# Rounding weight chunks two slots at a time in a one-core float32 decoder block

## The reference

```
def conv_gated_mlp(h, w_up, conv_w, conv_b, w_down):
    up = h @ w_up
    up = causal_depthwise_conv(up, conv_w) + conv_b
    gate, val = jnp.split(up, 2, axis=-1)
    return (jax.nn.silu(gate) * val) @ w_down

def reference(x, mem, ...):
    x = first_block(x, mem, w_in, w_out, ...)   # rmsnorm, attentions, recurrence, feed-forward
    return second_block(x, ..., w_in_2, ..., w_up_2, ..., w_down_2)   # mixers, feed-forward
```

## Time and profile before

| what | value |
| --- | --- |
| median of 3 runs | 2844.6 us |
| profiled execution: span from its first to its last instruction | 2844.7 us |
| TensorE busy with matmuls | 2734.1 us, 96% |
| VectorE, ScalarE, GpSimd busy | 64%, 43%, 9% |
| mean granted TensorE clock | 0.986 of full speed |
| DMA | 171 GB/s mean, 51.4% of 16 engines in the weights' queue |

### The profile page before, as it was taken

The page is one execution under the profiler, slowest core; times in us unless marked ns, Lnnn a source line. Parts: engine busy times, 40 slices in busy tenths (PEclk is TensorE's granted clock), DMA queues, the critical chain, the costliest instruction groups (busy, mean ns, idle before and its releaser), DMA issues.

```text
span 2844.7 us, 54953 instructions
## 1 busy us (share of the span) xinstructions
PE 2734.1 (96%) x21630; PEld 2679.8 (94%) x21630; DVE 1818.3 (64%) x2392; ACT 1235.6 (43%) x1532; POOL 252.6 (9%) x181
## 2 busy tenths in 40 slices
PE   7999969999999999999999999899899999999997
PEld 7989969998999999999999999889899999999997
DVE  6555785654544676867674547997576767676444
ACT  4344554434433444444443434534444444444332
POOL 3000001230001100000000304510310000000010
PEclk9999989999999999999999999999999999999998
DMA  6555423556534555555555555445455555555553
GB/s 214 193 178 162 151 67 134 194 179 192 185 127 154 178 179 185 178 188 180 177 190 182 184 185 162 146 162 173 133 163 187 183 178 185 182 184 182 184 185 105
DMA packets 131704, 485.67 MB, mean 171 GB/s; under 512 B 14765, under 2 KB 14773, under 8 KB 131152
## 3 DMA queue, kind: packets, MB, share of 16 engines
q1 hardware_dynamic: 129744, 474.01, 51.4%
q0 software_dynamic: 1792, 9.18, 0.9%
HBM read 481.02 MB, written 2.11 MB: 170 GB/s over the span
## 4 chain that ended last, share of the span: by engine, by line
PE 88%; DVE 7%; ACT 2%; issue 1%; POOL 1%; DMA 0%; ACTq 0%; SPq 0%; DVEq 0%; POOLq 0%
PE ps L1535 88%; DVE w_lo L919 2%; DVE acc L1348 1%; ACT w_hi L560 1%; DVE op_lo L965 1%; DVE hbuf L1504 1%; DMA raw<-in_weights 0%; DVE x_res L1507 0%; POOL sqb L495 0%; POOL sumsq L484 0%; POOL sumsq_w L484 0%; DVE proj L937 0%; POOL sqb L482 0%; DVE r_c L1099 0%; ACT hbuf L892 0%
## 5 line engine op out<-in xcount | busy, mean ns | idle before, releaser
L919 DVE TENSOR_TENSOR w_lo<-raw,w_hi 128x1024 fp32r<-128x1024 f32 x900 | 1129.3, 1263 | 926.4 <-ACT w_hi L560 924.1
L560 ACT ACTIVATE w_hi<-raw 128x1024 fp32r<-128x1024 f32 x900 | 951.0, 1060 | 1315.8 <-PE ps L1535 1287.6
L1535 PE MATMUL ps<-op_hi,w_hi 128*128 128x256 f32 x5024 | 1436.9, 286 | 54.8 <-DVE op_lo L965 28.3
L1535 PE MATMUL ps<-op_lo,w_hi 128*128 128x256 f32 x5024 | 1428.2, 284 | 0.0
L1535 PE MATMUL ps<-op_hi,w_lo 128*128 128x256 f32 x5024 | 1428.1, 284 | 0.0
L1535 PEld LDWEIGHTS ps<-op_hi,w_hi 128*128 128x128 f32 x5024 | 971.6, 193 | 61.8 <-DVE w_lo L919 47.4
L1535 PEld LDWEIGHTS ps<-op_lo,w_hi 128*128 128x128 f32 x5024 | 971.4, 193 | 0.8 <-issue 0.2
L1535 PEld LDWEIGHTS ps<-op_hi,w_lo 128*128 128x128 f32 x5024 | 971.0, 193 | 0.0
L1535 PE MATMUL ps<-g_lo,w_hi 128*128 128x256 f32 x1408 | 398.5, 283 | 0.0
L1535 PE MATMUL ps<-g_hi,w_lo 128*128 128x256 f32 x1408 | 397.8, 283 | 0.0
L1535 PE MATMUL ps<-g_hi,w_hi 128*128 128x256 f32 x1408 | 394.7, 280 | 0.0
(11 more groups left out here) (252 smaller groups left out, 1801.6 us busy)
## 6 DMA issues: line engine op xcount, KB each, us to landing
raw<-in_weights SPq DMA_DIRECT2D x900, 512.0 KB, 3.8
x_res<-in_x SPq DMA_DIRECT2D x1, 2048.0 KB, 8.3
x_res<-in_x POOLq DMA_DIRECT2D x1, 2048.0 KB, 7.8
mem_x<-in_mem POOLq DMA_DIRECT2D x1, 2048.0 KB, 10.3
out_x<-x_res POOLq DMA_DIRECT2D x8, 256.0 KB, 2.3
rel_rev<-rel_dram POOLq DMA_DIRECT2D x1, 1024.0 KB, 7.4
hg_con<-in_hg_consts POOLq DMA_DIRECT2D x1, 576.0 KB, 4.0
par<-in_params POOLq DMA_DIRECT2D x1, 546.0 KB, 9.4
```

The costliest lines, as they stand in the source:

```text
L560: nc.scalar.activation(w_hi[:, s], raw[:, s], ACT.Copy).then_inc(hi_rounded, 1)
L919: TT(w_lo[:, s], raw[:, s], w_hi[:, s].bitcast(F32), ALU.subtract).then_inc(chunk_split, 1)
L1535: return nc.tensor.matmul(out, lhsT, rhs, start=start, stop=stop, skip_group_check=True)
```

## The change

`split` on both engines now acts on two neighbouring slots. For the first four chunks of the program (`u` is the number 0) it is as before. After that it does nothing at even k; at odd k it waits for both loads and for both slots to be used up, and issues one instruction of 2048 columns for the pair, which raises its counter by 2. VectorE does the same for the rest. TensorE's and SyncE's programs are unchanged: they still wait for the count of their own chunk.

```
             def split(u, s):
-                act.wait_ge(raw_loaded[s], 16 * u + 16)
-                if not isinstance(u, int) or u > 0:
+                if isinstance(u, int) and u == 0:
+                    act.wait_ge(raw_loaded[s], 16)
+                    nc.scalar.activation(w_hi[:, s], raw[:, s], ACT.Copy).then_inc(hi_rounded, 1)
+                elif s % 2:
+                    for slot in (s - 1, s):
+                        act.wait_ge(raw_loaded[slot], 16 * u + 16)
                     act.wait_ge(chunk_used, SLOTS * u + (s - SLOTS + 1))
-                nc.scalar.activation(w_hi[:, s], raw[:, s], ACT.Copy).then_inc(hi_rounded, 1)
+                    nc.scalar.activation(w_hi[:, s - 1:s + 1], raw[:, s - 1:s + 1], ACT.Copy).then_inc(hi_rounded, 2)
...
             def split(u, s):
-                dve.wait_ge(hi_rounded, SLOTS * u + (s + 1))
-                TT(w_lo[:, s], raw[:, s], w_hi[:, s].bitcast(F32), ALU.subtract).then_inc(chunk_split, 1)
+                if isinstance(u, int) and u == 0:
+                    dve.wait_ge(hi_rounded, s + 1)
+                    TT(w_lo[:, s], raw[:, s], w_hi[:, s].bitcast(F32), ALU.subtract).then_inc(chunk_split, 1)
+                elif s % 2:
+                    dve.wait_ge(hi_rounded, SLOTS * u + (s + 1))
+                    pair = slice(s - 1, s + 1)
+                    TT(w_lo[:, pair], raw[:, pair], w_hi[:, pair].bitcast(F32), ALU.subtract).then_inc(chunk_split, 2)
```

## The result

The changed kernel takes 2890.7 us in the median of four runs (2886.09 to 2891.19) against 2844.4 us (2843.56 to 2844.92). The ratio is 1.0159, 95% interval 1.0145 to 1.0174: 46 us slower. The profiled execution's span grew from 2844.7 to 2889.0 us, by 44.3; the rest of this text divides up those 44.3. Every measured time is a median; one execution of experiment 6 took 12314 us and is left out.

The account below looks back on a forecast made before the run. TensorE's matmuls were taken to bound the kernel, filling 96% of the span, with splits hidden in spare time. Waits at listed places summed to 29.5 us on 2844.7, giving 2874 us, range 2851 to 2902.

Parts of the forecast that it names:

- Steady blocks at 0: `up`, `up_2`, `down`, `down_2` in their steady part: no loss, spare time never under 0.9 us.
- `da_fm`, +3.3: Start of the kernel: pair 10, 11 split at 57.5 us, so TensorE ends the block 3.3 us later.
- `hg_fm`, second block, +5.1: Attention: logits wait for an evacuation behind the pair's rest, +1.8; the logarithm ahead of chunks 12 and 13, +3.3.
- `out`, +4: Chunks 6 and 7 rounded ahead of the norm's operands, TensorE late for pair 8, 9, wait of 1.0 for 12, 13: +4.
- `mem_o`, +0.5: Evacuation now starts before a split and not behind it, and the rest is looser: +0.5 us.
- `conf`, `pool`, `gated`, +4: VectorE's lead capped at 1.45 us, so 2.9 more wait as GpSimd's taps slow it, 1.8 given back later: +4.
- Contention: Beside GpSimd's work, VectorE's loss stays one wait per GpSimd instruction, about 1.1 us, not growing with columns.
- rival worked out from columns: Beside GpSimd, loss grows with columns: another 1.1 us per pair, some 12 pairs, 2887 us; no separate chance given.
- Gated to `out_2`, +5: Normalisation steps +1.5, then `gated_hi(2)` stands before chunks 6 and 7 and TensorE waits 3.5: +5 us.
- Fewer instructions win: Rival: VectorE has less to do wherever TensorE waits for it, 2839 us; chance 0.05.
- The feed-forward breaks: Rival: the 0.9 us of spare time fails, about 1 us wait in each of 22 blocks, +22, 2896 us; chance 0.15.
- Mostly absorbed: Rival: TensorE's waits for operands, sums and attention steps cover the pairs at most places, +9, 2854 us; chance 0.14.

Follow-up runs that it names:

- experiment 6: The changed kernel with three ScalarE pieces (sigmoid and logarithm in `hg_fm`'s second block, `gated_hi(2)` in `out_2`) moved one chunk later, behind the pair; 2885.8 us.
- experiment 1: The changed kernel's places, waits and order, but each pair instruction split into two of 1024 columns; 2860.2 us, ratio 1.0059 to the kernel before.
- experiment 5: The change with pairs only in `up`, `down`, `up_2`, `down_2` behind their first blocks, single instructions elsewhere; 2850.2 us, ratio 1.0022 to the kernel before.
- experiment 11: The changed kernel with VectorE's second pair of evacuations ahead of the pair's rest at k = 5 of `hg_fm` and `mem_q`; 2881.6 us.
- Experiment 10: The kernel before, no pairs, with VectorE's evacuations of k = 4 and 5 ahead of the rest in `hg_fm`, `mem_q`, `mem_o`; 2837.1 us.
- experiment 7: The changed kernel with extra matmuls into an unused bank in `gated`'s first block, 50 before chunk 0 and 90 before chunk 10; 2888.7 us.
- experiment 9: The kernel before with 36, 34 and 70 extra matmuls before chunks 1, 4 and 10 of `gated`'s first block; 2843.8 us, ratio 1.0000.

## Why the prediction was right, and where it was short

The forecast, 2874 us with a range of 2851 to 2902, was that spare time is what the change spends and that it runs out at listed places. The sign and the mechanism hold, and the measured 2890.7 lies in the range; the sum of 29.5 us was too small by 15. The sum was one of waits, and TensorE's waits grew by 26.5 us in all; what it had nowhere are the 17.7 us by which TensorE's own work became slower.

- *Durations and spare time.* 1.92 and 2.3 us against 1.95 and 2.28; 1.35 us spare against 1.45. Right.
- *Steady blocks at 0.* Right for even blocks. Wrong by 4.4 us in the ten odd ones: "Spare time never falls under 0.9 us" counted the pieces and left out the table load of 1.28 us that stands ahead of a rounding there. It was in the trace of before, hidden. Experiments 1 and 5 show the term apart.
- *`da_fm`, +3.3.* It lost 4.6, by another path. The pair 10, 11 was split at 54.6 us, not at 57.5. TensorE waited 1.2 us for chunk 8, which the sum did not have, and 3.4 for chunk 10, and then took 4.6 us for chunk 10 in place of 2.9.
- *`hg_fm`, second block, +5.1.* The two waits came at the named places, and grew by 2.0 (costed 1.8) and 2.0 (3.3). The block lost 6.7, since the waits were followed by 1.5 and 1.7 us of matmuls at the lower clock. Experiments 6 and 11 remove one wait each and with it its clock.
- *`out`, +4.* It lost 6.5, at other places than those named; that the number is near is luck. The wait for the pair 8, 9 was 2.9 us where chunk 8 had waited 3.4 before, and none came for the pair 12, 13. The loss is 3.2 us in chunk 0, beside which the recurrence's steps come later, and 4.2 at chunk 6, which had 14 us of spare time before:

```profile
487.95 0.39 PE L1543 MATMUL ps<-op_hi,w_hi 128*128 128x256 f32 x1 [2.74 <-DVE w_lo L927]
```

The mean clock of the block fell from 0.91 to 0.86 as well.
- *`mem_q`, +1.9; `hg_fm`, third block, +1.7; `hg_i` and the first, +1; `up` and `up_2`, first block, +3.* 2.0, 2.8, 1.0 and 4.4. Right in place and sign.
- *`mem_o`, +0.5.* Wrong in sign: -2.5. "The evacuation now starts before a split and not behind it" was seen, and costed at the looser rest alone. TensorE's wait for `mq` there, 1.99 us before, is now 1.12, and the other 1.6 us are the slow matmuls behind it. Experiment 10 removes the wait altogether and turns this into the 6.8 us gain.

```profile
867.95 1.99 PE L1543 MATMUL ps<-mk,mq 128*128 128x256 f32 x8 [1.12 <-DVE mq L945]
```

- *`conf`, `pool`, `gated`, +4.* They lost 8.5: 4.9 in `conf` and `pool`, 5.4 in the first two blocks of `gated`, and 1.9 came back in its third. The wait at the last taps was 12 us (5.0 before), not 2.9 more than before with 1.8 given back. VectorE sets the pace, as argued, and the clock has little part in the loss (experiments 7 and 9). The 4.9 are 1.0 in `conf` 0, 2.2 in `conf` 1, where chunk 6 came 2.6 us late, and 0.9 each in `conf` 2 and `pool`, where the pair 4, 5 stood behind ScalarE's waiting piece, a place that the list did not have.
- *Contention.* In `gated` GpSimd's own taps (L535) run beside VectorE, without a break from 1882.8 to 1888.4 us. The rule of one wait per instruction held: wide rests took 3.35 us beside GpSimd against 2.28 alone, about as much more as a narrow one (2.32 against 1.23). In the changed kernel:

```profile
1887.19 3.35 DVE L927 TENSOR_TENSOR w_lo<-raw,w_hi 128x2048 fp32r<-128x2048 f32 x1
...
1893.48 2.28 DVE L927 TENSOR_TENSOR w_lo<-raw,w_hi 128x2048 fp32r<-128x2048 f32 x1
```

The Trainium skill, SBUF — State Buffer, section Who interferes with whom, has a VectorE instruction with two SBUF inputs and a GpSimd instruction that reads SBUF exclude each other for the whole instruction. The trace agrees with a price per instruction. The rival worked out from columns, 1.1 us more for each pair, is refuted. But fewer rests did not mean fewer collisions: the window sums of `gated` met GpSimd instead. A sum of 1024 columns took this in the changed kernel, 1.21 us in the one before:

```profile
1858.47 2.32 DVE L1402 TENSOR_TENSOR pa<-px 128x1024 f32<-128x1024 f32 x1
```

- *Gated to `out_2`, +5.* 5.8, with the wait at the chunk and behind the piece that were named. It was costed at 3.5 us and is 2.4, with 1.4 of slower matmuls behind it, so that the two errors cancel. Experiment 6 moves the piece and 4.2 us go.
- *The rivals.* "Fewer instructions win" needed waits under 3 us in all; there are 26 us more. "The feed-forward breaks" stayed far off its 22 us. "Mostly absorbed" gave +9 us, where even the kernel with narrow instructions (experiment 1) lost 16.

What stays open: why the first block, `da_fm`, loses 4.6 to 7.1 us with the same code in different kernels (predicted 3.3), and why VectorE split the last chunks of `gated` 0 3 us later when extra matmuls were added to the kernel before.

## What to carry to other kernels

Joining two instructions of a pipeline stage delays the first item of the pair by the whole second one. Ahead of the engine that sets the pace this is paid from spare time, so measure that spare time at the transitions and at each place with a long piece, not in the steady part: 408 chunks here took pairs for 6 us, the other 492 lost 40. Where an engine's list holds both look-ahead work and a result that someone waits for now, put the result first; that alone made the kernel before 6.8 us faster. And add to each new wait of the matmul engine the slower clock behind it, where nothing else sets the pace; in a stretch that another engine paces, it counts only behind the last wait.

## What the runs showed of the hardware

- Where TensorE alone sets the pace, stops of 2.8 and 2.05 us were followed by matmuls at a mean granted clock of 0.66 and 0.74, which cost 1.5 and 1.7 us on top. Where VectorE set the pace, a clock of 0.97 in place of 0.83 left the last pair at the same place (52.7 and 52.5 us into the block), and shortened only the two chunks behind it, from 8.3 to 6.1 us.
- 108 matmuls added in one block made TensorE stop for up to 2.3 us at the head of its loop in other blocks some 400 to 600 us later, six times, 18 us in all with the clock behind it; 140 added matmuls did not. At the stops the branch back took 4.0 to 4.2 us in place of 0.2, and 28 packets of instructions were loaded in this loop in place of 2 or 3. That the number added decides this by where the loop's instructions come to lie was argued, not shown; that the stops come and go with it was shown, in one kernel each. The Trainium skill, Runtime: NRT & Kernel Launch, section Instruction fetch mechanics, says that a taken branch whose target is not among the instructions that the engine holds stalls it for a fetch. The trace agrees, with the long branches and the packets beside them.
- The table load of 1.28 us recurs twice in every turn of ScalarE's loop, ahead of one rounding and ahead of the first `Silu` behind it. The load and the activations on both sides of it stand within 0.02 us of each other in the lines of `up` block 3.
